# Local attention of a streaming encoder layer: both parts of V in one weight load, the sink as a further score column, the halves added on VectorE, rounded on ScalarE, remainder on GpSimd

## The reference

```python
qa, ka, va, qb, kb, vb, gates = split_proj(rmsnorm(x, g_norm1), w_in)
oa = sink_attention(qa, ka, va, bias, sinks)     # local: 128 keys of window, whole chunks of 64
ob = stick_breaking(qb, kb, vb)                  # causal
merged = sigmoid(gates_a) * (oa @ w_proj_a) + sigmoid(gates_b) * (ob @ w_proj_b)
x = x + merged @ w_out
x = x + square(relu(rmsnorm(x, g_norm2) @ w_up)) @ w_down

def sink_attention(q, k, v, bias, sinks, valid=None):
    s = einsum('...qngd,...knd->...ngqk', q, k) * HEAD_DIM ** -0.5 + bias
    p = softmax(concatenate([s, sink], axis=-1), axis=-1)[..., :-1]
    return einsum('...ngqk,...knd->...qngd', p, v)
```

## Time and profile before

| quantity | value |
|---|---|
| median of three runs | 826.74 us |
| the profiled execution | 826.33 us |
| its span, first to last instruction | 824.5 us |
| TensorE busy | 813.7 us, 99% |
| VectorE busy | 618.9 us, 75% |
| ScalarE busy | 388.1 us, 47% |
| GpSimd busy | 295.2 us, 36% |
| mean granted TensorE clock | 0.998 of 2.4 GHz |
| first transpose of group 0 to the first product with V of group 19 | 63.45 to 139.30 us |

### The profile page before, as it was taken

How to read it: one execution, slowest core, us unless ns; L and a number is a source line. 1 busy time by engine, 2 the same in 40 slices (tenths; PEclk the granted TensorE clock), 3 DMA queues, 4 the chain that set the end, 5 groups by cost and what they waited for, 6 DMA issues and landing times.

```text
span 824.5 us, 15910 instructions
## 1 busy us (share of the span) xinstructions
PE 813.7 (99%) x6154; PEld 798.6 (97%) x6154; DVE 618.9 (75%) x1073; ACT 388.1 (47%) x668; POOL 295.2 (36%) x213
## 2 busy tenths in 40 slices
PE   9999999999999999999999999999999999999996
PEld 7999999999999999999999999999999999999995
DVE  4687876356879999876338988488966889488996
ACT  5657775244667758544342333233332333323532
POOL 2562222225545545344434300651035300552330
PEclk9999999999999999999999999999999999999999
DMA  9653112451112211143313113531134113412203
GB/s 285 240 165 99 52 52 66 153 166 52 53 53 87 65 51 51 51 169 125 103 55 100 52 52 104 153 102 53 51 107 147 51 51 102 147 57 78 75 2 115
DMA packets 68416, 78.16 MB, mean 95 GB/s; under 512 B 2536, under 2 KB 65040, under 8 KB 67984
## 3 DMA queue, kind: packets, MB, share of 16 engines
q1 hardware_dynamic: 68080, 76.92, 28.9%
q10 hardware_dynamic: 288, 0.60, 0.2%
HBM read 70.15 MB, written 8.93 MB: 96 GB/s over the span
## 4 chain that ended last, share of the span: by engine, by line
PE 91%; DVE 6%; issue 1%; ACT 1%; DMA 1%; DVEq 0%; SPq 0%; ACTq 0%
PE pan L1560 59%; PE pan L1775 12%; PE att L1775 11%; PE att L1713 1%; PE att L1686 1%; PE pan L1616 1%; PE att L1703 1%; PE att L1560 1%; DVE xT L1393 1%; DMA x_rows<-in_x_sample 1%; PE att L1855 1%; PE pan L1646 1%; DVE sq_sum L1492 0%; PE att L1742 0%; DVE x_out L1479 0%
## 5 line engine op out<-in xcount | busy, mean ns | idle before, releaser
L473 POOL TENSOR_TENSOR w_lo<-raw,w_hi 128x512 fp32r<-128x512 f32 x160 | 222.8, 1416 | 416.0 <-ACT w_hi L813 178.4
L1560 PE MATMUL pan<-a_hi,w_hi 128*128 128x288 f32 x624 | 134.0, 296 | 0.0
L1560 PE MATMUL pan<-a_lo,w_hi 128*128 128x288 f32 x624 | 133.4, 295 | 0.0
L1560 PE MATMUL pan<-a_hi,w_lo 128*128 128x288 f32 x624 | 132.8, 294 | 0.0
L1560 PE MATMUL pan<-h_lo,w_hi 128*128 128x288 f32 x512 | 109.5, 296 | 0.0
L1560 PE MATMUL pan<-h_hi,w_hi 128*128 128x288 f32 x512 | 109.4, 295 | 0.0
L1560 PE MATMUL pan<-h_hi,w_lo 128*128 128x288 f32 x512 | 108.8, 294 | 0.0
L1560 PEld LDWEIGHTS pan<-a_hi,w_hi 128*128 128x128 f32 x624 | 99.7, 188 | 1.0
L1560 PEld LDWEIGHTS pan<-a_hi,w_lo 128*128 128x128 f32 x624 | 100.0, 188 | 0.0
L1560 PEld LDWEIGHTS pan<-a_lo,w_hi 128*128 128x128 f32 x624 | 99.5, 188 | 0.0
L1775 PE MATMUL pan<-F_hi,w_hi 128*128 128x288 f32 x320 | 95.4, 298 | 0.6 <-DVE xT L1393 0.6
(11 more groups left out here) (279 smaller groups left out, 1750.5 us busy)
## 6 DMA issues: line engine op xcount, KB each, us to landing
raw<-in_w_in SPq DMA_DIRECT2D x34, 512.0 KB, 4.8
raw<-in_w_up SPq DMA_DIRECT2D x32, 512.0 KB, 4.5
raw<-in_w_down SPq DMA_DIRECT2D x32, 512.0 KB, 4.7
raw<-in_w_out SPq DMA_DIRECT2D x8, 512.0 KB, 4.1
x_spill<-xT SPq DMA_DIRECT2D x1, 2304.0 KB, 7.0
xT<-x_spill SPq DMA_DIRECT2D x1, 2304.0 KB, 10.4
x_rows<-in_x_prompt SPq DMA_DIRECT2D x4, 512.0 KB, 6.8
raw<-in_w_pa SPq DMA_DIRECT2D x4, 512.0 KB, 4.4
```

Of the source, the lines that this page charges most:

```text
L473: last = nc.gpsimd.tensor_tensor(w_lo[:, slot, k:k + 4, :], raw[:, rs, k:k + 4, j * P:(j + 1) * P], w_hi[:, slot, k:k + 4, :].bitcast(F32) ...
L1560: got = nc.tensor.matmul(out[:, h, 0:HALF], w, x[:, h * HALF:(h + 1) * HALF], start=first and n == 0, stop=last and n == 2)
```

## The change

`values` uses V hi and V lo side by side as one block of 128-wide weights, with P hi and P lo as the moving side: two matmuls for a block of keys in place of three. The product with V hi comes out in PSUM partitions 0 to 63, that with V lo in 64 to 127 (it now has the part V lo by P lo too). To join them, ScalarE copies the lower half to SBUF (`take_low`, 64 partitions x 256), VectorE adds it to the upper half into `oa_f` (two operations of 64x128 in place of four), ScalarE rounds `oa_f` one iteration later (`oa_high`, 128x128), and GpSimd takes the remainder (`oa_low`, 128x128). The sink becomes a column of the scores: VectorE copies it (128x2) ahead of the scores, the exponential runs over it too, and the two small exponentials and the addition to `den` go. GpSimd's loop over panels is written out for the panels that fall in the attention, so that `oa_low` can stand between the splits.

```diff
@@ gpsimd
+            def oa_low(g):
+                pair, t = g // 5, SW_ORDER[g % 5]
+                w, c0 = width(t), t * P
+                pool.wait_ge(swo_hi, g + 1)
+                nc.gpsimd.tensor_tensor(oa_lo[:, pair, c0:c0 + w], oa_f[:, g % 2, 0:w], oa_hi[:, pair, c0:c0 + w].bitcast(F32),
+                                        ALU.subtract).then_inc(oa_split, 1)
...
+            for g in range(SW_TILES):
+                for before, steps in ((SW_LEAD + 3 * g - 1, 1), (SW_LEAD + 3 * g, 2)):
+                    ended = sw_ended(before, steps)
+                    if ended:
+                        split_at(ended + 4)
+                if g:
+                    oa_low(g - 1)
+            oa_low(SW_TILES - 1)
@@ scalar
                 for e in range(2):
-                    nc.scalar.activation(s_sw[0:w, r, e, ks], s_sw[0:w, r, e, ks], ACT.Exp, bias=negm[0:w, r, e:e + 1], scale=-1.0,
-                                         accum_out=den[0:w, r, e:e + 1])
-                for e in range(2):
-                    last = nc.scalar.activation(snk[0:w, r, e:e + 1], nsink[0:w, 2 * pair + e:2 * pair + e + 1], ACT.Exp, bias=negm[0:w, r, e:e + 1], scale=-1.0)
+                    last = nc.scalar.activation(s_sw[0:w, r, e, ks], s_sw[0:w, r, e, ks], ACT.Exp, bias=negm[0:w, r, e:e + 1], scale=-1.0,
+                                                accum_out=den[0:w, r, e:e + 1])
...
+            def take_low(g):
+                w = width(SW_ORDER[g % 5])
+                act.wait_ge(swo_out, g + 1)
+                nc.scalar.activation(va_low[:, :, 0:w], att[HD:P, 3, 0:2 * P].rearrange("p (e n) -> p e n", e=2)[:, :, 0:w], ACT.Copy).then_inc(va_low_out, 1)
+            def oa_high(g):
+                pair, t = g // 5, SW_ORDER[g % 5]
+                w, c0 = width(t), t * P
+                act.wait_ge(swo_taken, g + 1)
+                nc.scalar.activation(oa_hi[:, pair, c0:c0 + w], oa_f[:, g % 2, 0:w], ACT.Copy).then_inc(swo_hi, 1)
...
                 ended = sw_ended(SW_LEAD + 3 * g, 2)
                 if ended:
                     round_at(ended + 4)
+                if g:
+                    oa_high(g - 1)
+                take_low(g)
@@ vector
+                nc.vector.tensor_copy(s_sw[0:w, r, :, 2 * P:2 * P + 1], nsink[0:w, 2 * pair:2 * pair + 2].unsqueeze(2))
                 dve.wait_ge(sc_out, g + 1)
...
                 dve.wait_ge(exp_ready, g + 1)
-                nc.vector.tensor_tensor(den[0:w, r, :], den[0:w, r, :], snk[0:w, r, :], ALU.add).then_inc(den_ready, 1)
-                dve.wait_ge(den_ready, g + 1)
                 nc.vector.reciprocal(rden[0:w, r, :], den[0:w, r, :]).then_inc(rden_ready, 1)
...
             def outputs(g):
-                dve.wait_ge(swo_out, g + 1)
-                for e in range(2):
-                    last = nc.vector.tensor_copy(oa_hi[e * HD:(e + 1) * HD, pair, c0:c0 + w], att[0:HD, 3, e * P:e * P + w])
-                last.then_inc(swo_hi, 1)
-                dve.wait_ge(swo_hi, g + 1)
-                for e in range(2):
-                    cols = oa_hi[e * HD:(e + 1) * HD, pair, c0:c0 + w]
-                    last = nc.vector.tensor_tensor(oa_lo[e * HD:(e + 1) * HD, pair, c0:c0 + w],
-                                                   att[0:HD, 3, e * P:e * P + w], cols.bitcast(F32), ALU.subtract)
+                dve.wait_ge(va_low_out, g + 1)
+                if g >= 2:
+                    dve.wait_ge(oa_split, g - 1)
+                for e in range(2):
+                    last = nc.vector.tensor_tensor(oa_f[e * HD:(e + 1) * HD, g % 2, 0:w], att[0:HD, 3, e * P:e * P + w], va_low[:, e, 0:w], ALU.add)
                 last.then_inc(swo_taken, 1)
@@ tensor
-                terms = [(*block, *parts) for block in key_blocks(t) for parts in ((0, pT_hi), (0, pT_lo), (1, pT_hi))]
-                for m, (kb, vt, kn, v_part, p_part) in enumerate(terms):
-                    got = nc.tensor.matmul(att[0:HD, 3, 0:256].rearrange("p (e n) -> p e n", e=2)[:, :, 0:width(t)],
-                                           va_st[0:kn, vt, g // 10, v_part, :], p_part[0:kn, r, 2 * kb:2 * kb + 2, 0:width(t)],
+                terms = [(*block, part) for block in key_blocks(t) for part in (pT_hi, pT_lo)]
+                for m, (kb, vt, kn, p_part) in enumerate(terms):
+                    got = nc.tensor.matmul(att[:, 3, 0:256].rearrange("p (e n) -> p e n", e=2)[:, :, 0:width(t)],
+                                           va_st[0:kn, vt, g // 10, :, :].rearrange("p a n -> p (a n)"), p_part[0:kn, r, 2 * kb:2 * kb + 2, 0:width(t)],
                                            start=m == 0, stop=m == len(terms) - 1)
...
+                if u == 0:
+                    pe.wait_ge(oa_split, SW_TILES)
                 half_panel(18 + 2 * u, 0, slot4(2 * u), oa_hi, oa_lo, middle=None if u else first_v_rows)
```

More of the change, by code:

```diff
@@ L47 @@
 KEYS = SEQ + WIN + NEW
+SWS = 2 * P + 4
 def width(t):
@@ L101, in build @@
         negm = keep("negm", [P, 2, 2])
-        snk = keep("snk", [P, 2, 2])
         den = keep("den", [P, 2, 2])
@@ L135, in build @@
         bias = work("bias", [P, SWH, 2 * P], 62272)
-        s_sw = work("s_sw", [P, 2, 2, 2 * P], 70464)
-        pT_hi = work("pT_hi", [P, 2, 4, P], 74560, F32R)
+        s_sw = work("s_sw", [P, 2, 2, SWS], 70464)
+        pT_hi = work("pT_hi", [P, 2, 4, P], 74624, F32R)
+        oa_f = work("oa_f", [P, 2, P], 78720)
+        va_low = work("va_low", [HD, 2, P], 79744)
         pT_lo = work("pT_lo", [P, 2, 4, P], 34592, F32R)
@@ L197, in build @@
         sw_staged, sc_out, max_ready = sem("sw_staged"), sem("sc_out"), sem("max_ready")
-        exp_ready, den_ready, rden_ready = sem("exp_ready"), sem("den_ready"), sem("rden_ready")
+        exp_ready, rden_ready = sem("exp_ready"), sem("rden_ready")
+        va_low_out, oa_split = sem("va_low_out"), sem("oa_split")
         qa_ready, bias_ready = sem("qa_ready"), sem("bias_ready")
@@ L227, in sw_cols, with sw_own @@
             return slice(0, WIN + NEW) if t == TT else slice(P, 2 * P) if t == 0 else slice(0, 2 * P)
+        def sw_own(t):
+            return slice(2 * P - WIN - NEW if t == TT else P if t == 0 else 0, 2 * P)
         def sw_first(t):
@@ L497, in stage_low, with split_at @@
                 pool.wait_ge(kq_ready, i * 2 + (q + 1))
-            with pool.Fori(0, 5) as b:
-                split_body(b, range(4))
+            def oa_low(g):
[4 more added lines that the diff above has]
+                                        ALU.subtract).then_inc(oa_split, 1)
+            def split_at(n):
+                split(n % 4, n // 2 % 2, n % 2, n + 1)
+            with pool.Fori(0, 2) as b:
+                split_body(b, range(4))
+            split_at(10)
+            for g in range(SW_TILES):
[6 more added lines that the diff above has]
+            oa_low(SW_TILES - 1)
+            for n in range(18, 22):
+                split_at(n)
             split_body(5, (0, 1, 2))
@@ L634, in exps @@
                 t, r = SW_ORDER[g % 5], g % 2
-                w, ks = width(t), sw_cols(t)
-                pair = g // 5
+                w, ks = width(t), slice(sw_own(t).start, 2 * P + 1)
                 act.wait_ge(max_ready, g + 1)
                 for e in range(2):
-                    nc.scalar.activation(s_sw[0:w, r, e, ks], s_sw[0:w, r, e, ks], ACT.Exp, bias=negm[0:w, r, e:e + 1], scale=-1.0,
-                                         accum_out=den[0:w, r, e:e + 1])
-                for e in range(2):
-                    last = nc.scalar.activation(snk[0:w, r, e:e + 1], nsink[0:w, 2 * pair + e:2 * pair + e + 1], ACT.Exp, bias=negm[0:w, r, e:e + 1], scale=-1.0)
+                    last = nc.scalar.activation(s_sw[0:w, r, e, ks], s_sw[0:w, r, e, ks], ACT.Exp, bias=negm[0:w, r, e:e + 1], scale=-1.0,
+                                                accum_out=den[0:w, r, e:e + 1])
                 last.then_inc(exp_ready, 1)
@@ L647, in normalise @@
                 t, r = SW_ORDER[g % 5], g % 2
-                w, ks = width(t), sw_cols(t)
+                w, ks = width(t), sw_own(t)
                 act.wait_ge(rden_ready, g + 1)
@@ L682, in _ @@
                     round_at(ended + 4)
+                if g:
+                    oa_high(g - 1)
+                take_low(g)
+            oa_high(SW_TILES - 1)
             round_at(18)
@@ L1041, in scores @@
                     last = nc.vector.tensor_tensor_reduce(
-                        out=s_sw[0:w, r, e, ks], in0=att[0:w, r, e * 256 + c0:e * 256 + c0 + ks.stop - ks.start],
+                        out=s_sw[0:w, r, e, own], in0=att[0:w, r, e * 256 + c0:e * 256 + c0 + ks.stop - ks.start],
                         in1=bias[0:w, 2 * pair + e, ks], scale=-1.0, scalar=nsink[0:w, 2 * pair + e:2 * pair + e + 1], op0=ALU.add, op1=ALU.min,
@@ L1069, in outputs @@
             def outputs(g):
-                pair, t = g // 5, SW_ORDER[g % 5]
-                w, c0 = width(t), t * P
-                dve.wait_ge(swo_out, g + 1)
```

(14 more changed lines are left out.)

3 lines of the change are left out of this document (2 added, 1 removed).

## The result

| | median us (runs) | against the kernel before | 95% interval |
|---|---|---|---|
| before | 827.02 (4) | 1 | |
| after | 832.6 (4) | 1.0067 | 1.0049 to 1.0084 |

The changed kernel is 5.6 us slower. The forecast was +3.9 us to 830.6, in a range from 825.0 to 832.8, so the measured 832.6 lies just inside its upper end. The profiled execution of the changed kernel took 833.5 us, with a span of 831.5.

What follows compares the result with a forecast made beforehand. Bound: a closed loop through ScalarE and VectorE instead of PE. Loops 61.5, panels' ends 4.7 + 1.5, held copies 3.5, the end 0.67 + 3.35: 75.2 us against 70.99; net +3.9 us to 830.6, range 825.0 to 832.8.

Steps and rivals of the forecast that it cites:

- The bound changes from PE to a loop: Attention stage: `pT_low` to `pT_low` through ScalarE and VectorE sets the time, 3.42 to 3.91 us a round without panels' ends.
- PE's waits for `pT_low`: Sign in the timeline after: PE waits at L1713 in most groups from 2 on, some 7 us in all.
- PE's part: Products with V: fewer matmuls at unchanged spacing take 3.3 us off PE, bounds 3.2 and 3.6.
- The panels' ends inside the loop: Weight roundings lengthen the loop by 5 x 0.94 = 4.7 us, and `take_qkv` by 2 x 0.73 = 1.5.
- The held copy: VectorE's sink copy is held by GpSimd's split after iterations 1, 6, 9, 14: 3.5 us, bounds 0 and 3.5.
- the loop binds, but the copy isn't held: Rival: loop sets the time without held sink copies, 3.5 us lower, +0.4 us to 827.1; chance 0.28.
- `oa_high(g - 1)`, 128x128 ... so 0.19: ScalarE's rounding ahead of `take_low(g)` adds 0.19 us to each loop, 0.12 for a sample; bounds 0.15 and 0.30.
- The copy's own 0.08: VectorE's copy of the sink ahead of the scores, when not held, adds 0.08 us per loop; upper bound 0.20.
- The total: From `pT_low(1)` to group 19's first product 75.2 us, 4.2 more than now; net +3.9 us, chance 0.44.
- the loop is longer than worked out: Rival: sink copy 0.20 and 0.03 more for the rounding, in 16 iterations, 2.4 us more, 833.0; chance 0.14.
- The wider weights save nothing: Rival: four 128-wide products take as long as six 64-wide; forecast hardly changes; chance counted within a 0.28.
- PE keeps the pace: Rival: ScalarE and VectorE stay ahead of PE, so the 3.3 us come out, 823.4; chance 0.14.

Runs made afterwards that it cites:

- The third product: `pT_hi` multiplied a second time with the same weights, in the changed kernel (834.9 us, ratio 1.0078) and in the kernel with its queues reordered (829.81 us, 1.0026).
- the wide weights alone: The kernel before with only the matmuls changed to two 128-wide products per block of keys, halves not joined: 826.21 us, ratio 0.9970.
- `oa_high` early: The changed kernel with `oa_high(g - 1)` moved from ahead of `take_low(g)` to right behind `take_pT(g)`: 832.36 us, ratio 1.0049.
- the reordered ones: The changed kernel with ScalarE, VectorE and GpSimd work in another order: 825.82 us, 0.9976; with the sink's copy also ahead of `pT_low`: 824.37 us, 0.9963.

## Why the prediction was right, and where it was off

**The bound changes from PE to a loop: right.** The round of tile 2 without a panel's end was forecast at 3.66 us; after, `pT_low` of groups 8 and 9 starts 102.85 - 99.09 = 3.76 apart. The next round (tile 3), with a panel's end in it, took 4.47 (to 107.32) for 3.42 + 0.94 = 4.36, and the one behind it (a sample), with a held copy, 4.32 (to 111.64) for 3.44 + 0.98 = 4.42. The third product, nearly free in one kernel and at most of its price in the other, shows the bound by itself. PE's waits for `pT_low` were forecast at some 7 us in most groups; PE shows 5.4 us in ten, and its weight loads 7.8.

**PE's part: 3.3 us forecast, 2.5 measured** by the wide weights alone. A period of five groups shrank by 0.72 us instead of 0.82, because the sample's products got 0.04 longer instead of staying equal and one tile's gain fell short, and 0.2 more is PE's wait. In the changed kernel it counts only in the last two groups, behind the last `pT_low` of the loop: 0.18 us each for a forecast 0.23.

**The panels' ends inside the loop: right.** Roundings measured 0.95 each against 0.94, and the round with `take_qkv` in iteration 12 took 4.74, 0.74 more than the round of iteration 2 less its hold (4.61 - 0.61), against 0.73. With the roundings moved out of the loop, and the holds gone with them, the stage got 7.2 us shorter.

**The held copy: right in kind, too large.** Forecast 0.77 twice and 0.98 twice, sum 3.5; measured 0.61 twice and 0.76 and 0.77, and one of 0.13 beyond them, sum 2.9. The holds are shorter for two reasons of about the same size: the copy came 0.07 to 0.14 us later behind the rounding than worked out (1.97 and 1.83 for 1.90 and 1.69, with the rounding taken as 0.94), and the operation behind it started some 0.06 before the split's record ended (74.82 for 74.88), where 0.03 behind it was worked out. The rival "the loop binds, but the copy isn't held" fell.

**The step that was mis-sized is "`oa_high(g - 1)`, 128x128 ... so 0.19", with "bounds 0.15 and 0.30".** It measured 0.32 from its start to that of `take_low` (76.74 to 77.06), and 0.26 for a sample's half width where 0.12 was forecast: 0.13 a round over seventeen rounds, 2.2 us, a little outside my upper bound. The rows from which it came had one PSUM-sourced rounding behind another. The same operation takes 0.20 to 0.22 to the next one where that reads SBUF (77.72 to 77.94 in the kernel with `oa_high` early). So most of the excess depends on what stands behind the operation, here `take_low`. Why is open. That `take_low` reads PSUM and waits for PE isn't enough: in the kernel before `take_pT` does both, and at 102.84 it started 0.10 us before the record ahead of it ended. ScalarE's timeline before:

```profile
101.90 1.04 ACT L557 ACTIVATE w_hi<-raw 128x1024 fp32r<-128x1024 f32 x1
```

**The copy's own 0.08** was 0.06: 0.3 us less over the stage. In sum 71.2 us were forecast from `pT_low(1)` to `pT_low(18)` and 141.25 - 68.90 = 72.35 measured: +2.2 for `oa_high`, -0.6 for the holds, -0.3 for the copies come to +1.3 against the +1.15 found.

**The total.** The stage gave +5.5 for +4.2 forecast, less 0.2 for the last group: 5.3 of the 5.6 us between the medians. The rest is inside the interval of the ratio (1.0049 to 1.0084 is 4.1 to 6.9 us). There is some luck in the number: the errors of +2.2 us and of -0.9 us had opposite signs, and without the second the time would have been above the range. The measured 832.6 is nearer to the rival "the loop is longer than worked out" (833.0) than to the forecast, though not for its reason: that rival made the copy 0.12 us dearer, and it was cheaper, and the rounding 0.03, and it was 0.13.

"The wider weights save nothing" fell by the wide weights alone, 2.5 us faster. "PE keeps the pace" needed each round 0.22 shorter and no holds. That wasn't so in the changed kernel; in the reordered ones PE waits once or not at all, and by their ratios they are at 824.8 and 823.7 on the prediction's scale, near its 823.4.

## What to carry to other kernels

Before a wait is moved from one engine to another, write down both queues and follow the cycle from an instruction back to itself: a step that gives an engine less work can close a loop through two in-order queues, whose length, not anybody's busy time, then sets the pace. Put what nobody waits for soon (roundings for a later panel, high parts of finished outputs, constants) out of that cycle, and keep a small VectorE copy between SBUF tiles where it can be held behind a GpSimd operation without anyone waiting. A matmul taken away is worth its time only where the engine is still the bound: doubling the doubtful work, in both orders, is a cheap way to know.

## What the runs showed of the hardware

- A VectorE copy of two columns from SBUF to SBUF, 0.15 us alone, that started inside an operation of GpSimd with more than that left of it ended 0.02 to 0.03 us behind that operation, in the traces of all kernels that have it: up to 1.22 us long inside a split, 0.32 inside an `oa_low`. The one exception started 0.02 us behind the start of a split and took 0.16. Copies of one column were never held (146 ns at most in forty, sixteen of them inside an operation of GpSimd). An addition of 128x2 with both inputs in SBUF was held too (0.87 for 0.16), a reciprocal of 128x2 wasn't (0.17 inside a split).
- On ScalarE `oa_hi` starts 0.09 to 0.10 us before the end of the record ahead of it (76.65 + 0.19 against 76.74), and `take_low` and the `take_pT` behind it 0.02 to 0.03 us after it (76.74 + 0.29 against 77.06; with `oa_high` early, 76.69 + 0.38 against 77.10). In the kernel before `take_pT` started 0.10 before it (101.90 + 1.04 against 102.84). So neither a PSUM source nor the wait for PE makes the 0.11 us by itself, and what does was not found.
- At 256 columns weights of 128 and of 64 columns give the same spacing, 0.12 us a matmul; at 128 columns four wide matmuls took 0.63 us, six narrow ones 0.59.
